# One row of norm weights spread by TensorE, and a logarithm that takes the sum of squares itself

## The reference, cut to what matters

```python
def rms_norm(x, gain):
    xf = x.astype(jnp.float32)
    y = xf * lax.rsqrt(jnp.mean(xf * xf, axis=-1, keepdims=True) + NORM_EPS)
    return (y * gain.astype(jnp.float32)).astype(x.dtype)
...
        hp = rms_norm(y_prompt, norm_pre[l])
        mp, st_p = mixers_prompt(hp, w_in[l], attn_sinks[l], rel_bias[l], slopes)
        y_prompt = y_prompt + rms_norm(jnp.einsum('btm,md->btd', mp, w_out[l]), norm_post[l])
        hs = rms_norm(y_sample, norm_pre[l])
```

## Time and profile before

| | before |
|---|---|
| median of 3 runs | 1939.57 us (1939.03 to 1939.63) |
| profiled execution, first to last instruction | 1936.8 us |
| what lies around the span, by the median | 2.8 us |
| PE busy | 1905.3 us (98%) |
| DVE busy | 1240.0 us (64%) |
| ACT busy | 666.4 us (34%) |
| POOL busy | 53.3 us (3%) |
| granted TensorE clock, mean | 0.997 |

### The profile page before, as it was taken

How to read it: one execution, slowest core, us unless ns; L and a number is a source line. 1 busy time by engine, 2 the same in 40 slices (tenths; PEclk the granted TensorE clock), 3 DMA queues, 4 the chain that set the end, 5 groups by cost and what they waited for, 6 DMA issues and landing times.

```text
span 1936.8 us, 30940 instructions
## 1 busy us (share of the span) xinstructions
PE 1905.3 (98%) x12508; PEld 1746.7 (90%) x12508; DVE 1240.0 (64%) x2224; ACT 666.4 (34%) x1257; POOL 53.3 (3%) x119
## 2 busy tenths in 40 slices
PE   6999999999999999999999999999999999999997
PEld 5999999999999999999999999999999988888886
DVE  7358777787878778553544454355525566766878
ACT  7124233343433334222222222233213354344453
POOL 4000000000000000000000000000000000000131
PEclk9999999999999999999999999999999999999999
DMA  6456777676777767666657667465446657555396
GB/s 245 117 120 137 159 157 165 145 147 154 146 162 154 162 146 149 151 137 136 149 119 155 141 136 143 104 141 123 106 97 144 136 197 278 192 175 187 121 258 226
DMA packets 880407, 301.05 MB, mean 155 GB/s; under 512 B 618504, under 2 KB 845592, under 8 KB 878968
## 3 DMA queue, kind: packets, MB, share of 16 engines
q1 hardware_dynamic: 877192, 290.35, 61.6%
q0 software_dynamic: 3072, 8.73, 2.2%
HBM read 210.45 MB, written 96.20 MB: 158 GB/s over the span
## 4 chain that ended last, share of the span: by engine, by line
PE 86%; DVE 9%; DMA 1%; ACT 1%; issue 1%; POOL 0%; SPq 0%; DVEq 0%; ACTq 0%; POOLq 0%
PE ps L1204 21%; PE ps L1205 20%; PE ps L1206 20%; PE ps L1400 4%; PE ps L1401 4%; PE ps L1402 4%; PE ps L1292 3%; PE ps L1371 3%; PE ps L1264 2%; PE ps L1342 2%; DVE arena L1853 1%; DVE act_lo L1740 1%; DVE arena L1733 1%; DMA b_out<-in_w_out_dram 1%; DVE arena L1841 1%
## 5 line engine op out<-in xcount | busy, mean ns | idle before, releaser
L1204 PE MATMUL ps<-act_hi,w_hi 128*128 128x352 f32 x2688 | 878.8, 327 | 0.1
L1206 PE MATMUL ps<-act_hi,w_lo 128*128 128x352 f32 x2688 | 863.7, 321 | 0.0
L1205 PE MATMUL ps<-act_lo,w_hi 128*128 128x352 f32 x2688 | 863.6, 321 | 0.0
L1204 PEld LDWEIGHTS ps<-act_hi,w_hi 128*128 128x128 f32 x2688 | 505.2, 188 | 24.7 <-issue 20.7
L1205 PEld LDWEIGHTS ps<-act_lo,w_hi 128*128 128x128 f32 x2688 | 506.1, 188 | 0.0
L1206 PEld LDWEIGHTS ps<-act_hi,w_lo 128*128 128x128 f32 x2688 | 504.9, 188 | 0.0
L1501 ACT ACTIVATE w_hi<-w_raw 128x512 fp32r<-128x512 f32 x224 | 139.3, 623 | 340.5 <-DMA w_raw<-in_w_in_dram 340.4
L1748 DVE TENSOR_TENSOR w_lo<-w_raw,w_hi 128x512 fp32r<-128x512 f32 x224 | 150.9, 675 | 51.5 <-ACT w_hi L1501 51.2
L1568 ACT ACTIVATE arena<-arena,small 128x257 f32<-128x257 f32 (+6 forms) x180 | 101.3, 565 | 209.1 <-DVE small L1891 209.1
L2079 DVE STREAM_TRANSPOSE arena<-arena 128x1024 f32<-128x1024 f32 (+4 forms) x100 | 132.6, 1326 | 40.0 <-ACT arena L1691 39.2
L1691 ACT ACTIVATE arena<-arena 128x1024 f32<-128x1024 f32 (+1 forms) x60 | 61.0, 1017 | 255.8 <-DVE arena L1865 255.7
(11 more groups left out here) (182 smaller groups left out, 2105.5 us busy)
## 6 DMA issues: line engine op xcount, KB each, us to landing
w_raw<-in_w_in_dram SPq DMA_DIRECT2D x176, 256.0 KB, 3.3
weight_scratch<-arena SPq DMA_DIRECT2D x216, 128.0 KB, 3.4
arena<-weight_scratch SPq DMA_DIRECT2D x54, 512.0 KB, 4.5
b_out<-in_w_out_dram SPq DMA_DIRECT2D x72, 256.0 KB, 3.3
w_raw<-in_w_out_dram SPq DMA_DIRECT2D x70, 256.0 KB, 2.7
w_raw<-in_w_in_dram SPq DMA_DIRECT2D x96, 128.0 KB, 3.1
weight_scratch<-arena SPq DMA_DIRECT2D x80, 132.0 KB, 4.1
arena<-weight_scratch SPq DMA_DIRECT2D x40, 256.0 KB, 3.3
```

Source lines behind the costliest of these rows:

```text
L1204: mm(bank(g, GN), wh, ah, start=(k == 0), stop=False)
L1205: mm(bank(g, GN), wh, al, start=False, stop=False)
L1206: last = mm(bank(g, GN), wl, ah, start=False, stop=(k == KT - 1))
```

## The change

The gain now comes as one row of 8 KB into partition 0 (`gain_row`, which lies in the buffer of `w_hi`), and this load is issued behind the first tile of x instead of behind the second. DVE first writes 128 ones (`ones_row`) and a column with EPS (`eps_at`). PE, ahead of its wait for the constants, does four matmuls of the ones (one row, 128 columns) with 512 floats of the row each, into the banks 3 to 6. DVE copies each bank into `pre_gain`, and then does `x_scale(0)`. The two small copies for the bias table move behind `x_scale(0)`.

Ln reads `ssq` with scale 1/D and EPS as its bias, in all nine tiles, so it waits for ACT's own sum and no longer for POOL's var. POOL still makes var for the Newton step; it waits for its own var now, and for the last Newton step ahead of the next.

```diff
+        gain_row = place("gain_row", [P, D], F32, 0, ring0 + RING * PIECE)
+        ones_row = arena[0:1, 12480:12480 + P]
+        eps_at = small[:, 18:19]
...
-                if t == 1:
-                    sp.dma_start(pre_gain, norm_pre[0].partition_broadcast(P)).then_inc(gain_in, 16)
+                if t == 0:
+                    sp.dma_start(gain_row[0:1, :], norm_pre[0:1]).then_inc(gain_in, 16)
...
+            pe.wait_ge(ones_made, 1)
+            pe.wait_ge(gain_in, 16)
+            for g in range(4):
+                mm(bank(X + g), ones_row, gain_row[0:1, PIECE * g:PIECE * g + PIECE], start=True, stop=True).then_inc(gain_spread, 1)
             pe.wait_ge(consts, CONSTS)
...
-                act.wait_ge(x_var, t + 1)
-                fn(r, var[0:rows, t:t + 1], ACT.Ln).then_inc(x_ln, 1)
+                act.wait_ge(x_sq, t + 1)
+                if t == 0:
+                    act.wait_ge(eps_made, 1)
+                fn(r, ssq[0:rows, t:t + 1], ACT.Ln, bias=eps_at[0:rows, :], scale=1.0 / D).then_inc(x_ln, 1)
...
+            v.memset(ones_row, 1.0).then_inc(ones_made, 1)
+            v.memset(eps_at, EPS).then_inc(eps_made, 1)
             v.memset(qbd[:, :], 0.0).then_inc(zeroed, 1)
-            dve.wait_ge(rel_in, 16)
-            v.tensor_copy(ext[:, 0:P], tab[:, 2 * CLIP:2 * CLIP + 1].broadcast_to([H_C, P])).then_inc(ext_made, 1)
-            v.tensor_copy(ext[:, P:P + 2 * CLIP], tab[:, 2 * CLIP - 1::-1]).then_inc(ext_made, 1)
-            dve.wait_ge(gain_in, 16)
+            for g in range(4):
+                dve.wait_ge(gain_spread, g + 1)
+                v.tensor_copy(pre_gain[:, PIECE * g:PIECE * g + PIECE], bank(X + g)).then_inc(gain_made, 1)
+            dve.wait_ge(gain_made, 4)
...
+            x_scale(0)
+            dve.wait_ge(rel_in, 16)
+            v.tensor_copy(ext[:, 0:P], tab[:, 2 * CLIP:2 * CLIP + 1].broadcast_to([H_C, P])).then_inc(ext_made, 1)
+            v.tensor_copy(ext[:, P:P + 2 * CLIP], tab[:, 2 * CLIP - 1::-1]).then_inc(ext_made, 1)
...
-            x_scale(0)
             for t in range(TT + 1):
...
                 pool.wait_ge(x_std, t + 1)
+                if t:
+                    pool.wait_ge(x_rstd, 4 * t)
                 gp.tensor_tensor(nt, r, r, ALU.mult).then_inc(x_rstd, 1)
+                pool.wait_ge(x_var, t + 1)
                 pool.wait_ge(x_rstd, 4 * t + 1)
```

More of the change, by code:

```diff
@@ L761, in build @@
         x_in = [sem(f"x_in{i}") for i in range(4)]
-        gain_in = sem("gain_in")
+        gain_in, gain_spread, gain_made = sem("gain_in"), sem("gain_spread"), sem("gain_made")
+        ones_made, eps_made = sem("ones_made"), sem("eps_made")
         x_sq, x_var, x_ln, x_std, x_rstd, x_norm = (sem(n) for n in ("x_sq", "x_var", "x_ln", "x_std", "x_rstd", "x_norm"))
```

## The result

| | before | after |
|---|---|---|
| median of 15 runs | 1939.43 us (1938.13 to 1941.22) | 1943.13 us (1941.98 to 1944.87) |
| ratio | | 1.0020, 95% interval 1.0013 to 1.0027 |
| profiled execution, span | 1936.8 us | 1941.1 us |

The change makes the kernel 3.7 us slower. The forecast was 1941.2 us, the range 1938.8 to 1943.0: the sign was right, the forecast loss of 1.65 us was under half of what was measured, and the median lies 0.1 us above the range. The time around the span is 1.7 us in the changed kernel's profiled execution; the 2.8 us of before came from setting one execution's span against the median of others, so that execution was some 1 us faster than its median. The changed kernel's was 0.3 us faster than its own.

The account below looks back on a forecast made before the run. DVE was taken to bound the first stage, PE what follows 54 us. Matmuls, copies and moved copies put `x_scale(1)` at 15.6 to 15.7 instead of 14.02 us: 1939.57 + 1.65 = 1941.2 us, range 1938.8 to 1943.0.

Parts of the forecast that it names:

- (2): PE's four gain matmuls: slow until the clock rises 4.8 us after their start, from 6.05 to 12.1 us; bounds 9.7 to 13.2.
- Where the bound is: DVE bounds the first stage, dense from `x_scale(1)` at 14.02 us; its shift passes on, PE being the bound after 54 us.
- (7): First transposes from 15.3 us, 3.65 us at the low level; `x_low(0)` at about 18.0, DVE dense from `x_scale(1)` on.
- (1): Load of the 8 KB gain row behind tile 0: landed at 5.9 us, bounds 5.6 to 8.1; tile 1 at most 0.3 later.
- Rival C: PE's clock does not rise for matmuls of a single row: +2.7 us, 1942.3 us; chance 0.14.
- (3): DVE's four gain copies from PSUM, 0.68 us each, only the last on the path; `x_scale(0)` starts at 12.9 us.
- (4): Ln starts 0.3 us earlier per tile, tile 0's Newton step done at about 9.2 instead of 9.47 us; worth nothing.
- (5): Tile 1's Newton step on POOL done at about 12.1 us, before `x_scale(0)` can hold it; L2137's 2.05 us stall goes.
- (6): The two small copies, now between `x_scale(0)` and `x_scale(1)` on DVE, lose their idle-time cover: +0.43 us.

Follow-up runs that it names:

- late_before: Kernel before, with a wait for ACT's copies and two unused PSUM copies on DVE behind `x_scale(1)`, a pure delay: 1942.04 us against 1938.75, ratio 1.0019.
- full_rows: Changed kernel with the spreading over all 128 rows, zeros outside partition 0 cleared by DVE: 1940.18 us against 1938.99, ratio 1.0005.
- warm1: Changed kernel with ten one-row bf16 products of 512 columns on PE ahead of the spreading: 1940.38 us against 1938.75, ratio 1.0008.
- ln_only: Kernel before with only the Ln's new form, the gain still broadcast by DMA: 1938.90 us against 1938.99, ratio 1.0002.
- warm128: Changed kernel with ten 128-row bf16 products of 512 columns on PE ahead of the spreading: 1937.96 us against 1938.75, ratio 0.9999.
- copies_back: Changed kernel with the two small bias-table copies ahead of the gain copies again: 1942.39 us against 1938.73, ratio 1.0020.
- best: Changed kernel with 128-row warm-up products, spreading over all rows and the small copies ahead again: 1938.09 us against 1938.73, ratio 0.9994.

## Why the prediction was wrong in size

Two steps failed. The first is term (2), which took the clock to rise during the one-row products. The second is the sentence "everything behind is tied to it by semaphores, and after 54 us PE is the bound and starts that much sooner or later", which left no room for a loss behind the start. By the first alone the time would have come to about 1942.1 us, within the range.

- Where the bound is: right. DVE was the bound from `x_scale(1)` on but for the 0.2 us of (7), and the delay of its start was passed on (late_before: 2.84 us given, 3.3 measured, with an interval of 1.9 to 5.4).
- (1) The row's load: right. First product at 5.95 us, forecast 6.05. Tile 1's squares started at 8.45, 0.15 us late, off the path.
- (2) The matmuls: this is the term that was mis-sized. Taken was 6.05 us, from 6.05 to 12.1; measured 7.17 us, from 5.95 to 13.12. The price of a pass was right, 0.85 us at the low level. What failed is the sentence "I take 4.8, since this is again the first work of PE": the 4.8 us were read from transposes of 128 rows. The prediction took it that the clock rises from products of one row as from those. full_rows shows that it would have (some 5 us with all rows), warm1 that it doesn't in 11.4 us of one row. Rival C had the cause and 13.2 us for the end of the products, and was given 0.14.
- (3) The copies: right, 0.69 us each, `x_scale(0)` 0.76 us behind the last product, forecast 0.8.
- (4) The Ln: right that it is worth nothing, wrong in its own size. With scale and with its bias from a column, Ln takes 0.29 instead of 0.20 us, and POOL's extra wait adds 0.07 between its first two instructions. Tile 0's step ended at 9.46, as before, not at 9.2, with the tile's squares 0.1 us later (5.73 instead of 5.63): some 0.1 us was saved and not 0.3. ln_only says the same, 9.29 with squares from 5.56.
- (5) The stall of L2137: right. POOL's four instructions took 0.19 us each and ended at 12.17, forecast 12.1, three of them starting beside a gain copy (11.44, 11.71 and 11.98 within 11.44 to 12.13). This is the point for which no row of before stood: a copy out of PSUM does not hold POOL. The trace agrees with the rule of the Trainium skill ("SBUF — State Buffer", Who interferes with whom) that was weighed there; beside `x_scale`, an instruction of this step takes 2.27 us in warm128 (the third) and 2.23 us in ln_only (the first) again.
- (6) The moved copies: between `x_scale(0)` and `x_scale(1)` as forecast, +0.34 us instead of 0.43; by themselves worth nothing (copies_back).
- (7) The transposes: missed by 0.2 us. With `x_scale(1)` right behind `x_scale(0)` there was less room for the 3.66 us of slow transposes than the sentence reckoned, and `x_low(0)` waited.
- What remained beyond the start, 1.1 us: no step had it. The runs show that two kernels of the same course differ there by 2 us, repeatably: in the changed kernel PE loses 2.8 us between 330 and 884 us in waits for the value tile and gains 0.9 at 1608 us. What makes these waits come and go is open. Half a microsecond for each unknown was too little for the upper end; with C at 1942.3 and this rest on top, 1943.4 was within what could come.

By the terms: 2.62 us from the start (1.65 forecast; 1.0 of the difference is the clock) and 1.1 from what lies behind it.

## What to carry to other kernels

A broadcast by products with ones on a single row ran at the low clock here, for as long as it lasted (11.4 us in warm1), and it let a clock that was up fall again (warm128). Where it is on the path, use all rows (zeros in the others, whose clearing took 1.76 us ahead of the load) and let PE do full products before it, or reckon with 1.7 us for each 512 fp32 columns. Before taking a transfer off the path, look what holds the step behind it: here `x_scale(1)` hung on POOL, not on the gain, so that even the spreading at full clock (best) brought `x_scale(1)` only 0.16 us forward. And do not read a difference of 1 or 2 us in 1940 as the work of an edit before the same edit has been timed with a harmless instruction more or less.

## What the runs showed of the hardware that was not expected

- TensorE's clock falls while PE is busy without a pause, when its products use one row: 1.00, 0.65, 0.50 granted in three successive microseconds of warm128, PE busy 1.00 in each. With 128 rows the same passes raise it after some 5 us from rest (full_rows), and after ten bf16 products of 128 rows from 1.54 us on it stayed up through all of full-row spreading (best, 3.67 us).
- The granted clock in the windows is 1.00 over the first microseconds also where passes take twice their time (the changed kernel, 6 to 13 us): there the pace of the passes tells the level, not that column.
- One VectorE instruction of 0.48 us, on no path, moved the whole run by 1.6 to 1.9 us; an unused semaphore did not (+3.97 us with it, +3.70 and +3.81 without).
